# Hybrid decoder trunk: opening transfers, full-row small products, and another order in the attention stage

## The reference

```python
for l in range(DEPTH):                                   # DEPTH = 2
    h = rms_norm(x, attn_norm[l])
    x = x + token_mix(h, ...)                            # one projection w_in, three mixers, one w_out
    h = rms_norm(x, mlp_norm[l])
    x = x + jnp.square(jax.nn.relu(h @ w_up)) @ w_down   # 1024 -> 4096 -> 1024

# token_mix: proj = h @ w_in is split into the inputs of three mixers
#   GLA: gated linear attention in chunks of 64, 4 heads (64 keys, 128 values), normalised, times silu(gate)
#   DSA: an indexer scores keys, sum_h iw * relu(iq . ik); each query keeps its best 128 causal keys; softmax over them, 4 heads of 64
#   MLA: queries and keys from low-rank latents (192 and 128), rotary on 32 of 96, dense causal softmax, 4 heads
#   out = concatenate([o_gla, o_dsa, o_mla]) @ w_out
```

## Time and profile before

| | |
|---|---|
| median of 3 runs | 1266.64 us (1266.44 to 1268.1) |
| profiled execution | 1267.81 us, its span 1264.6 us |
| PE busy | 1238.2 us, 98% of the span |
| DVE, ACT, POOL busy | 754.1, 526.9, 216.0 us |
| moved by transfers | 108.34 MB, 86 GB/s on average |
| layer 0: opening to first attention product, attention, first output product | 0 to 180.05, to 240.47 |
| layer 1: the same stages | begin 625 us later |

### The profile page before, as it was taken

How to read it: one execution, slowest core, us unless ns; L and a number is a source line. 1 busy time by engine, 2 the same in 40 slices (tenths; PEclk the granted TensorE clock), 3 DMA queues, 4 the chain that set the end, 5 groups by cost and what they waited for, 6 DMA issues and landing times.

```text
span 1264.6 us, 17596 instructions
## 1 busy us (share of the span) xinstructions
PE 1238.2 (98%) x5924; PEld 967.1 (76%) x5924; DVE 754.1 (60%) x1231; ACT 526.9 (42%) x853; POOL 216.0 (17%) x139
## 2 busy tenths in 40 slices
PE   6999999999999999999999999999999999999998
PEld 5766776688888888888886668757888888888887
DVE  5689877654554544554756888685445445444444
ACT  5574347744214223234436644486442232332331
POOL 1122340021120110210521323300201102102002
PEclk9999999999999999999999999999999999999999
DMA  6221220033222322222222112201322222232233
GB/s 227 84 67 51 79 89 1 1 100 130 96 90 97 100 99 88 99 95 100 100 83 84 59 59 84 67 1 34 100 83 100 95 90 98 100 100 100 88 98 113
DMA packets 29999, 108.34 MB, mean 86 GB/s; under 512 B 3456, under 2 KB 3456, under 8 KB 29952
## 3 DMA queue, kind: packets, MB, share of 16 engines
q1 hardware_dynamic: 28800, 102.77, 24.3%
q0 software_dynamic: 720, 3.90, 0.8%
q10 hardware_dynamic: 432, 1.07, 0.3%
HBM read 105.64 MB, written 2.10 MB: 85 GB/s over the span
## 4 chain that ended last, share of the span: by engine, by line
PE 90%; DVE 4%; ACT 3%; issue 2%; DMA 1%; DVEq 0%; POOL 0%; ACTq 0%; POOLq 0%
PE bank L850 18%; PE bank L851 18%; PE bank L849 18%; PE bank L486 6%; PE bank L488 6%; PE bank L487 6%; PE bank L507 2%; PE bank L509 2%; PE bank L508 2%; PE bank L520 2%; PE bank L732 1%; PE bank L744 1%; DVE pb L1537 1%; PE bank L759 1%; DMA x<-in_x 1%
## 5 line engine op out<-in xcount | busy, mean ns | idle before, releaser
L904 ACT ACTIVATE wh<-raw 128x1024 fp32r<-128x1024 f32 x192 | 202.6, 1055 | 379.9 <-PE bank L851 246.3
L1211 DVE TENSOR_TENSOR wl<-raw,wh 128x1024 fp32r<-128x1024 f32 x156 | 242.5, 1555 | 73.5 <-ACT wh L904 73.5
L849 PE MATMUL bank<-hh,wl 128*128 128x512 f32 x512 | 200.0, 391 | 0.0
L849 PE MATMUL bank<-xmh,wl 128*128 128x512 f32 x512 | 199.3, 389 | 0.0
L851 PE MATMUL bank<-hl,wh 128*128 128x512 f32 x512 | 199.2, 389 | 0.0
L850 PE MATMUL bank<-xmh,wh 128*128 128x512 f32 x512 | 199.2, 389 | 0.0
L851 PE MATMUL bank<-xml,wh 128*128 128x512 f32 x512 | 199.2, 389 | 0.0
L850 PE MATMUL bank<-hh,wh 128*128 128x512 f32 x512 | 199.2, 389 | 0.0
L453 POOL TENSOR_TENSOR x<-x,rsb 128x512 f32<-128x512 f32 x63 | 83.3, 1321 | 589.2 <-DVE rsb L1627 589.2
L486 PE MATMUL bank<-xgh,wl 128*128 128x512 f32 x368 | 150.5, 409 | 11.6 <-DVE xgl L1219 11.6
L1616 DVE TENSOR_TENSOR sqb<-tf 128x512 f32<-128x512 f32 x64 | 44.3, 692 | 181.7 <-ACT hh L1179 181.7
(11 more groups left out here) (196 smaller groups left out, 1627.9 us busy)
## 6 DMA issues: line engine op xcount, KB each, us to landing
raw<-in_stream SPq DMA_DIRECT2D x192, 512.0 KB, 3.3
out_y<-x SPq DMA_DIRECT2D x8, 256.0 KB, 3.6
x<-in_x ACTq DMA_DIRECT2D x2, 512.0 KB, 7.8
x<-in_x POOLq DMA_DIRECT2D x2, 512.0 KB, 9.8
con<-in_consts POOLq DMA_DIRECT2D x1, 976.5 KB, 4.9
par<-in_params POOLq DMA_DIRECT2D x1, 916.0 KB, 4.9
par<-in_params POOLq DMA_DIRECT2D x1, 896.0 KB, 6.5
par<-in_params ACTq DMA_DIRECT2D x1, 20.0 KB, 2.4
```

What stands on the lines that cost most here:

```text
L849: pe.matmul(B.t[s][:], wl[:, s, n_block(k)], src_h[:, k], start=(k == 0), stop=False)
L904: act.activation(wh[:, s], raw[:, s], ACT.Copy).then_inc(hi_ready.sem, 1)
L1211: vec.tensor_tensor(wl[:, s], raw[:, s], wh[:, s], ALU.subtract).then_inc(lo_ready.sem, 1)
```

## The change

Seven edits:

1. Opening, layer 0: the first weight tile comes in two halves and x in eight single blocks, from the queues of SP and ACT; 16 products of `ones` with itself go ahead; the eight squares go to free tiles, behind unit 1's split.
2. The total of the squares and the transpositions for `rcol` stand one unit (and one dv block) later, in other banks; VectorE reads iq0 and iq1 later.
3. Products with 16, 32 or 64 rows become products with 128, the rest of the rows zero (`glrs`, `cqn`, `low_rows`, `turn_rows`); POOL clears two tiles per layer.
4. `relevance(5)` moves from ahead of unit 9 into its middle.
5. `gvt` is copied by ScalarE alone; `masked_scores` 1 and 0 stand behind the first and second half of the states.
6. Gates 2 and 3 move from steps 13 and 14 to 27 and 28, `MIXED` is reordered accordingly, and five blocks instead of three of output unit 1 stand ahead of unit 0's last one.
7. The sparse logits move from even steps (four ahead, behind the even step's transposition) to odd steps (three ahead, right ahead of the weighing), in other banks.

```diff
-MIXED = [0, 1, 2, 3, 6, 7, 4, 5]
+MIXED = [0, 1, 6, 7, 2, 3, 4, 5]
+MIX_OF = [("gla", 0), ("gla", 1), ("out", 0), ("out", 1), ("gla", 2), ("gla", 3), ("out", 2), ("out", 3), ("out", 4)]
+WARM = 16
-GATE_SLOT = {6: 0, 7: 1, 13: 2, 14: 3}
+GATE_SLOT = {6: 0, 7: 1, 27: 2, 28: 3}
-PAIR_LEAD = 4
+PAIR_LEAD = 3
...
-    if _j % 2 == 0 and _j + PAIR_LEAD < N_ATT:
-        TAIL += [(f"lg{i}", (2, 3, 6, 7)[i % 4]) for i in (_j + PAIR_LEAD, _j + PAIR_LEAD + 1)]
+    if _j % 2 == 1 and _j + PAIR_LEAD < N_ATT:
+        TAIL += [(f"lg{i}", (3, 7, 2, 6)[i % 4]) for i in (_j + PAIR_LEAD, _j + PAIR_LEAD + 1)]
...
+            sp.dma_start(raw[:, 0, 0:T], stream[0][:, 0:T]).then_inc(half_loaded, 16)
+            sp.dma_start(raw[:, 0, T:2 * T], stream[0][:, T:2 * T]).then_inc(raw_loaded[0], 16)
+            for d in (2, 4, 6, 7):
+                sp.dma_start(x[:, d], x_in[:, d]).then_inc(x_loaded[d], 16)
+            sp.dma_start(raw[:, 1], stream[1]).then_inc(raw_loaded[1], 16)
...
+                pool.memset(glrs[:], 0.0).then_inc(padded.sem, 1)
+                pool.memset(cqn[QK:P, 1], 0.0).then_inc(padded.sem, 1)
...
+            for _ in range(WARM):
+                pe.matmul(B.t[3][:, 0:P], ones[:], ones[:], start=True, stop=True)
...
-                    pe.matmul(B[name][:], par[0:64, c:c + P], cqn[0:64, 1], start=False, stop=True)\
+                    pe.matmul(B[name][:], par[:, c:c + P], cqn[:, 1], start=False, stop=True)\
...
-                    pe.matmul(B[name][:], ones[64:QK, :], cqn[64:QK, 1], start=False, stop=True)\
+                    pe.matmul(B[name][:], turn_rows[:], cqn[:, 1], start=False, stop=True)\
...
-                relevance(5)
-                unit(9)
+                unit(9, before=midway(5))
...
+                    if j % 2 == 1 and N_MLA <= j + PAIR_LEAD < N_ATT:
+                        logits_pair(j + PAIR_LEAD)
                     if j >= LAG and (j - LAG) % 2 == 1:
                         weigh_pair(j - LAG - 1)
-                    if j % 2 == 0 and N_MLA <= j + PAIR_LEAD < N_ATT:
-                        logits_pair(j + PAIR_LEAD)
...
-                first_out(1, 0, 3)
+                first_out(1, 0, 5)
                 first_out(0, KB - 1, KB)
-                first_out(1, 3, KB)
+                first_out(1, 5, KB)
...
-                        for tb in range(2):
+                        for tb in range(TB):
                             act.wait_ge(*B.filled(l, f"gv{tb}"))
...
-                masked_scores(0)
-                masked_scores(1)
...
                 states(0, 0)
+                masked_scores(1)
                 states(0, 1)
+                masked_scores(0)
```

More of the change, by code:

```diff
@@ L489, in feature_unit, with token_units @@
                 m.then_inc(*B.on_fill(name))
-            def token_units(l, u0, blocks, width, stem):
+            def token_units(l, u0, blocks, width, stem, between=None):
                 for i, (ka, kb) in enumerate(blocks):
@@ L515, in token_units @@
                         m.then_inc(token_spent.sem, 1)
+                    if i == 0 and between is not None:
+                        between()
             def stat(l, name, lhsT, rhs, rows=P, cols=slice(0, T)):
@@ L585, in _, with column_factor @@
                 unit(1)
+                unit(2)
                 total("xstat", 0)
[L587 to L593 removed]
+                def column_factor():
+                    pe.wait_ge(*rb_ready.at(l, 0))
+                    pe.wait_ge(*B.vacant(l, "rcol"))
+                    for tb in range(TB):
+                        m = pe.transpose(B["rcol"][:, tb * P:(tb + 1) * P], rb[:, tb * P:(tb + 1) * P], ident)
+                    m.then_inc(*B.on_fill("rcol"))
+                token_units(l, 3, DV_BLOCKS, DVW, "dv", between=column_factor)
                 pe.wait_ge(*B.freed(l, "iq1"))
@@ L630, in _ @@
                 pe.wait_ge(*B.vacant(l, "cqst"))
+                pe.wait_ge(*rows_ready.at(0, 4))
                 pe.matmul(B["cqst"][:], ones[:], sqb[:, 0], start=True, stop=False)
-                pe.matmul(B["cqst"][:], ones[0:64, :], lnb[0:64], start=False, stop=True)\
+                pe.matmul(B["cqst"][:], low_rows[:], lnb[:], start=False, stop=True)\
                     .then_inc(*B.on_fill("cqst"))
                 stat(l, "ckvst", ones[:], sq_of("ckvst"))
-                relevance(5)
-                unit(9)
+                unit(9, before=midway(5))
                 stat(l, "dqst0", blk, sq_of("dqst0"))
@@ L922, in gained, with opening_squares @@
                 squared(l, half, k)
-            split(0, 1)
-            act.wait_ge(gains_loaded, 16)
-            for k in range(0, KB, 2):
-                act.wait_ge(x_loaded[k // 2], 16)
+            def opening_squares(first, last):
+                for k in range(first, last):
+                    act.activation(opening_square(k), x[:, k], ACT.Square).then_inc(sq_ready.sem, 1)
+            act.wait_ge(half_loaded, 16)
+            act.activation(wh[:, 0, 0:T], raw[:, 0, 0:T], ACT.Copy).then_inc(half_high.sem, 1)
+            act.wait_ge(gains_loaded, 16)
+            for k in range(KB):
+                if k == 1:
+                    act.wait_ge(raw_loaded[0], 16)
+                    act.activation(wh[:, 0, T:2 * T], raw[:, 0, T:2 * T], ACT.Copy).then_inc(hi_ready.sem, 1)
+                act.wait_ge(x_loaded[k], 16)
                 gained_high(k, xgh, G_ATTN)
-                gained_high(k + 1, xgh, G_ATTN)
-                if k in (0, 2):
-                    squared(0, 0, k)
-                    squared(0, 0, k + 1)
             split(1, 1)
-            for k in range(4, KB):
-                squared(0, 0, k)
+            opening_squares(0, 4)
+            act.wait_ge(*unit_done(0, 0))
+            split(0, 2)
+            opening_squares(4, KB)
             act.wait_ge(const_loaded, 16)
@@ L1396, in evacuations @@
                         evacuate(f"gg{u - 16}", gg[:, u - 16])
-                    if u == 23:
-                        for tb in range(2, TB):
-                            vec.wait_ge(*B.filled(l, f"gv{tb}"))
-                            vec.tensor_scalar(gvt[:, tb], B[f"gv{tb}"][:], rcol[:, tb:tb + 1], None, ALU.mult)\
-                                .then_inc(*B.on_read(f"gv{tb}"))
                 def tasks(u):
@@ L1465, in _ @@
                 for u in range(N_IN):
-                    if u not in POOL_LOW:
+                    if u not in POOL_LOW and (l, u) != (0, 0):
                         low_part(u % 2, hi_ready.at(l, u + AHEAD))
```

146 lines of the change are left out of this document (88 added, 58 removed).

## The result

The changed kernel takes 1271.89 us (median of 6 runs, 1270.35 to 1273.13) against 1266.61 before: ratio 1.0041, 95% interval 1.0028 to 1.0054. It is slower by 5.3 us, where 1259.5 was forecast.

What follows compares the result with a forecast made beforehand. TensorE, busy 98% of the span, was taken as the bound. Terms -4.0 - 3.4 + 0 - 0.9 + 0.8 + 0.4 = -7.1, off the median 1266.64, gave 1259.5 us, range 1256.4 to 1262.9.

Steps and rivals of the forecast that it cites:

- the sparse half: Attention's sparse steps: 0.9 gained by step 25, used up by late normalisations; +0.8 us for both layers, bounds -2.4 and +2.8.
- The late gates: Sparse half: moving gates 2 and 3 takes 2.9 us off VectorE, which come back from step 27 on.
- The lead: Sparse half: logits one transposition less ahead, in other banks; the 0.99 wait at logits 16 goes, step 25 still 0.9 earlier.
- The first rival: Sparse half: late gates are hidden and the gain is kept, -1.2 per layer instead of +0.4, 1256.3; chance 0.16.
- The slower rival: Sparse half: with two transpositions back to back, each of nine pairs waits 0.75, twice: +13.5, 1273; chance 0.04.
- Start of attention: Before the first transposition: VectorE rid of gvt copies and masked scores, 0.45 per layer; -0.9, bounds 0 and -1.5.
- Full rows: Small full-precision products: filling rows with zeros saves 0.28 at six places per layer; -3.4, bounds 0 and -3.9.
- Opening: Layer 0's start: smaller transfers and reordered work bring unit 1 from 18.11 to 14.1; -4.0, bounds -5.3 and -2.5.
- Relevance(5): Moved into unit 9: its 1.13 us stall only reappears before dqst0's statistic; 0, bounds -2.3 and +0.2.
- Output units: Six products more ahead save 0.4, but out2 waits 0.6 for its weights; +0.4 for both layers, bounds -0.8 and +1.2.

Runs made afterwards that it cites:

- logits_even: Changed kernel with the sparse logits back at even steps, four ahead, behind the weighing, in their old banks; late gates kept: 1262.8 us, ratio 0.9958.
- even_gates_early: logits_even with gates 2 and 3 also back at steps 13 and 14 and the old order of blocks in the output units: 1263.4 us, ratio 0.9976.
- vec_order: Changed kernel with, on VectorE at odd steps of the sparse half, normalise(j+2) ahead of mask_max(j+3): 1273.5 us, ratio 1.0050.
- lead_five: Changed kernel with the sparse logits five steps ahead instead of three, still at odd steps and in the new banks: 1268.4 us, ratio 1.0014.
- gvt_split: Changed kernel with gvt 2 and 3 copied by VectorE again; masked scores still between the states: 1270.5 us, ratio 1.0032.
- narrow_rows: Changed kernel with operands of the small products cut back to 64, 32 and 16 rows, zero rows still made: 1276.1 us, ratio 1.0069.
- best_masks: Changed kernel with even logits four ahead, late gates, states(0,0) ahead of normalise(0), masked scores first, three blocks of output unit 1 ahead: 1256.5 us, ratio 0.9920.
- best_between: As best_masks, but with the masked scores between and behind the halves of the states, as in the changed kernel: 1257.0 us, ratio 0.9921.
- norm_behind: Changed kernel with two VectorE calls exchanged, states(0,0) ahead of normalise(0): 1268.9 us, ratio 1.0023.

## Why the prediction was wrong

**The step that failed** is the one on the sparse half, "Against it stands the lead of one transposition less. Worked through ..., the weighing of step 25 starts 0.9 earlier than today". With the late gates it was to give +0.8; it gave +7.8. From the first weighing to that of step 25 layer 0 takes 40.55 us before, 43.98 in the changed kernel, 3.4 later, and 39.20 with the old lead (logits_even). The two halves of the term had opposite fates.

- *The late gates*: I let their 2.9 us come back at the end and eat the gain. They gain 1.1 / 0.8 us per layer net (even_gates_early); the end takes back 0.3 in layer 0, where I had 1.3. The first rival (-1.2 per layer) had the mechanism and the size.
- *The lead*: the logits' move costs 5.0 us per layer (logits_even). The pair comes one transposition later, but VectorE's queue has mask_max(j+3) ahead of normalise(j+2), and ScalarE's has exponential j+3 ahead of turned j+1, so one late pair of logits holds back work that was ready (rows 221.29 to 224.01 for VectorE; ScalarE's part is read from its order and wasn't tried alone). To exchange the two on VectorE does not help (vec_order): the loop from logits to transposition needs the distance itself, which lead_five and logits_even give back. My sum followed durations, which say that three steps of TensorE are long enough, and not what stands behind a waiting instruction in each queue. I gained the 0.99 at logits 16, as forecast, and got eight waits of 0.67 on average.

**The slower rival** named the place and the price nearly: it decides "from 0.53 per pair on", and the waits are 0.67; it put the loss at 13.5 us, and logits_even puts it at 10.0. It had 0.04, since I held that logits and weighing between pairs give VectorE time to catch up. They do, with a lead of four or five; its own cause, two transpositions back to back, is not the cause (lead_five keeps them so and waits 0.6 us).

**Start of attention**: -0.9 forecast, +3.2 measured. "The masked scores come back between and behind the halves of the states" costs 0.46 per layer and not nothing. That ScalarE takes the gvt copies "0.6 behind TensorE's end, which delays its split" was seen and not followed on: the split releases POOL's subtraction, and this holds VectorE's normalisation, 0.57 per layer (gvt_split). The trace of before already showed the pair, a normalisation of 0.67 us that ends with POOL's instruction. The rest, 1.15 in one layer of the profile, is the clock.

**Full rows**: mechanism right, term too small: -4.5 in the stretch (4.5 come back in it with narrow_rows, 4.2 in the median) for -3.4. I counted the narrow product (0.19) and the switch to it (0.09). The switch back is the third piece: from mla_q's first product to the second product of the next unit it is 81.74 (that product's start in the trace of before) - 79.40 = 2.34 before and 78.54 - 76.59 = 1.95 now, 0.39 and not 0.28; 6 x 2 x 0.39 = 4.7. The Trainium skill ("TensorE: Matmul & The Clock Gate", its table on why this matters, small-K row) gives a single product with 32 rows the time of one with 128. The rows and narrow_rows show otherwise: 1.05 for 32 rows (124.18) beside 0.86.

**Opening**: mechanism right, term too large: -2.7 for -4.0. The running total of bytes told when all would be there (ScalarE's last wait for x ends at 9.85, and I had x[7] at 9.9), not when x[0] would: 6.37 instead of 4.2. VectorE, behind ScalarE, so ends its last xgl at 14.10 instead of 12.0. ScalarE's four issues took 2.41 us, 0.6 each and not 0.45, and its table load ended at 4.91 instead of 4.3; x[0] came later than that. The warm-up products weren't tried alone.

**Relevance(5)**: 0, as forecast, with the wait where it was said to go (1.62 for 1.5). **Output units**: +1.6 for +0.4. Out2's cover of nine products was counted right, and its weights too; what ends last is the bank, read by VectorE behind the low part (254.82, 0.68 us). With three blocks ahead the stretch is 46.0 again (best_masks).

Forecast: -4.0 - 3.4 + 0 - 0.9 + 0.8 + 0.4 = -7.1. Measured: -2.7 - 4.5 - 0.2 + 3.2 + 7.8 + 1.6 = +5.2.

## What to carry to other kernels

When work is moved later in one engine's order, go through each other queue and ask what stands behind the instruction that will now wait, and how many steps of lead the whole loop has left; durations alone said that three steps were enough. Where one stage has both a change that helps (late gates) and one that hurts, undo them one at a time: here the better half gives about 2 us once the other half is undone, and with that, with the masks and the last output blocks back in place and one pair of calls exchanged, the whole change is worth 0.8% instead of costing 0.4%. And an idle time of TensorE ahead of a dense stretch can cost more than its own length: here 1.6 us, and in some executions 1.15 us more behind it.

## What the runs showed of the hardware that I had not expected

- **The granted clock can fall behind a short idle time on the path.** In the changed kernel TensorE idles 1.6 us before the first transposition, and in some layers the next 3 us run at 1.2 GHz (granted clock 0.50, window 0.56): the 28 products take 2.88 instead of 1.75 us, and the stretch is 12.0 instead of 10.84, 1.15 more. Of eight profiles with this idle time it fell in one layer in five, in both in one and in none in two; never there in a profile with 1.02 or 0.87 us, and not with the idle time filled. It isn't the same in each execution: the changed kernel's run with a mean clock of 1.000 took 1270.35, those with 0.997 took 1272.91 and 1273.13, which is most of its spread of 2.8 us. The idle time alone does not decide: TensorE waits 1.6 us before dqst0's statistic too (row 75.66), in both layers of twelve of these profiles, and the clock never fell there. What else it takes is not shown. In vec_order and best_between it fell once between the layers (in the latter to 0.52 from 637.0 to 640.5, behind gaps of 0.86 and 0.71 us that stand in the kernel of before as well, without a fall in its profile), and two of best_between's five runs are 1.4 to 1.6 us above the rest.
- **VectorE waits for POOL.** A 128x128 multiply from SBUF to SBUF, 0.29 us elsewhere, took 1.55 and 1.75 us beside POOL's subtraction and ended within 0.1 us of it, while masks and states that read PSUM kept their length beside it. The Trainium skill ("SBUF — State Buffer", on the two separate sides) says that VectorE and GpSimd share one pair of ports, which an instruction holds for its whole length, and that VectorE wants it only in a two-port mode or with two inputs in SBUF. By that rule the states, with at most one input in SBUF, need not wait, and the trace of norm_behind agrees (0.29 and 0.37 us each beside POOL). Whether the multiply runs in such a mode no row shows; that it waits, its 1.55 us do.
- **A product with few rows costs on both sides, but not with 96.** A product of 64 rows among full ones costs TensorE 0.39 us more than one of 128 rows with zeros: 0.09 ahead of it, 0.19 in it, 0.11 behind it. One of 32 rows took as long as one of 64 (1.05 us). One of 96 rows and 96 columns between full ones starts 0.86 us before the next, like a full one (86.98 to 87.84 in the earlier trace rows). Why 96 differs wasn't tried.
